# Two transformer blocks on one core: index scores issued in pairs of heads, four more weight loads whose low halves come by transfer, and block 2's memory attention with its outputs laid out by features

## The reference, cut to what matters

```python
    for layer in range(DEPTH):
        h = rmsnorm_2(x, norm_mix[layer])
        hq, hf, hi, hg, sq, sk, sv, iq, ik, iw, mq = split_in(h @ w_in[layer])
        o_hg = hgrn2_mix(hq, hf, hi, hg, lb[layer], hg_out_gain[layer])
        o_sa = dsa_mix(sq, sk, sv, iq, ik, iw, sa_q_gain[layer], sa_k_gain[layer])
        o_mem = mem_mix(mq, rmsnorm_2(mem, norm_mem[layer]), w_mem_kv[layer],
                        mem_q_gain[layer], mem_k_gain[layer])
        x = x + jnp.concatenate([o_hg, o_sa, o_mem], -1) @ w_out[layer]

# dsa_mix, for each block of 128 queries
        s = jnp.einsum('bqhd,bsd->bqhs', iqb, ik32)
        score = jnp.einsum('bqh,bqhs->bqs', iwb, jax.nn.relu(s))
# mem_mix
    logits = jnp.einsum('bqhd,bmhd->bhqm', qm, km) * (MEM_DH_2 ** -0.5)
    p = jax.nn.softmax(logits, axis=-1)
    out = jnp.einsum('bhqm,bmhd->bqhd', p, vm)
```

## Time and profile before

| | |
|---|---|
| median of 3 runs | 1542.08 us (1541.72 to 1542.87) |
| the profiled execution, its time | 1541.8 us |
| the profiled execution, its span | 1540.0 us |
| TensorE busy | 1521.7 us, 99% |
| VectorE busy | 860.6 us, 56% |
| ScalarE busy | 641.3 us, 42% |
| GpSimd busy | 24.1 us, 2% |
| DMA, mean | 103 GB/s |

### The profile page before, as it was taken

One profiled execution on the slowest core, in us unless ns is written; L12 is line 12 of the kernel. 1 busy time (PEld: TensorE's weight loads), 2 busy tenths in 40 slices (PEclk: granted clock), 3 DMA queues, 4 the chain that ended last, 5 costly groups with the idle time before them and its releaser, 6 DMA issues. The chain is left out here.

```text
span 1540.0 us, 20083 instructions
## 1 busy us (share of the span) xinstructions
PE 1521.7 (99%) x7670; PEld 1268.5 (82%) x7670; DVE 860.6 (56%) x1321; ACT 641.3 (42%) x888; POOL 24.1 (2%) x32
## 2 busy tenths in 40 slices
PE   7999999999999999999999999999999999999999
PEld 7888667888888888888888868999888888888887
DVE  5443565444456877777434778878564543444222
ACT  6442444322245444444333555686653322322210
POOL 0000000000000000000000000010000000000000
PEclk9999999999999999999999999999999999999999
DMA  9313212232233133222333223254312322222232
GB/s 363 132 55 109 103 56 82 83 109 94 98 113 133 55 110 109 83 107 82 137 109 128 69 83 113 56 124 106 91 65 82 110 84 107 87 103 96 95 109 82
DMA packets 25386, 158.33 MB, mean 103 GB/s; under 512 B 2819, under 2 KB 3331, under 8 KB 8300
## 3 DMA queue, kind: packets, MB, share of 16 engines
q1 hardware_dynamic: 23228, 150.01, 27.5%
q0 software_dynamic: 2016, 7.34, 2.5%
q10 hardware_dynamic: 80, 0.13, 0.0%
HBM read 147.87 MB, written 2.13 MB: 97 GB/s over the span
## 5 line engine op out<-in xcount | busy, mean ns | idle before, releaser
L1202 DVE TENSOR_TENSOR w_lo<-raw,w_hi 128x2048 fp32r<-128x2048 f32 x109 | 249.8, 2292 | 347.3 <-ACT w_hi L644 347.2
L1952 PE MATMUL bank<-h_hi,w_hi 128*128 128x512 f32 x1096 | 431.5, 394 | 1.1 <-DVE cy L1544 0.8
L1954 PE MATMUL bank<-h_hi,w_lo 128*128 128x512 f32 x1096 | 427.0, 390 | 0.0
L1953 PE MATMUL bank<-h_lo,w_hi 128*128 128x512 f32 x1096 | 426.7, 389 | 0.0
L644 ACT ACTIVATE w_hi<-raw 128x2048 fp32r<-128x2048 f32 x123 | 235.0, 1910 | 321.7 <-PE bank L1954 307.4
L1952 PEld LDWEIGHTS bank<-h_hi,w_hi 128*128 128x128 f32 x1096 | 205.6, 188 | 45.3 <-issue 2.8
L1954 PEld LDWEIGHTS bank<-h_hi,w_lo 128*128 128x128 f32 x1096 | 205.3, 187 | 43.7
L1953 PEld LDWEIGHTS bank<-h_lo,w_hi 128*128 128x128 f32 x1096 | 205.5, 188 | 42.0 <-issue 0.2
L1952 PE MATMUL bank<-a_hi,w_hi 128*128 128x512 f32 x352 | 136.9, 389 | 0.0
L1953 PE MATMUL bank<-a_lo,w_hi 128*128 128x512 f32 x352 | 136.9, 389 | 0.0
L1954 PE MATMUL bank<-a_hi,w_lo 128*128 128x512 f32 x352 | 136.9, 389 | 0.0
(11 more groups left out here) (315 smaller groups left out, 2005.2 us busy)
## 6 DMA issues: line engine op xcount, KB each, us to landing
raw<-weights SPq DMA_DIRECT2D x128, 1024.0 KB, 4.8
w_lo<-raw POOLq DMA_DIRECT2D x14, 512.0 KB, 5.0
toep<-bias_scratch SPq DMA_DIRECT2D x8, 448.0 KB, 4.6
x<-xT SPq DMA_DIRECT2D x2, 1024.0 KB, 12.7
x_tok<-x_tok SPq DMA_DIRECT2D x1, 2048.0 KB, 13.8
mem2T<-mem2T SPq DMA_DIRECT2D x2, 1024.0 KB, 5.3
outT<-x SPq DMA_DIRECT2D x8, 256.0 KB, 4.2
lead<-lead SPq DMA_DIRECT2D x2, 512.0 KB, 4.7
```

Source lines behind the costliest of these rows:

```text
L1202: nc.vector.tensor_tensor(w_lo[PLACE[m]][:, :], raw[m % 2][:, :], w_hi[PLACE[m]][:, :].bitcast(F32), ALU.subtract).then_inc(lo_ready, 1)
L1952: nc.tensor.matmul(o, lh, rh, start=first, stop=False)
L1953: nc.tensor.matmul(o, lh, rl, start=False, stop=False)
L1954: return nc.tensor.matmul(o, ll, rh, start=False, stop=last)
```

## The change

- `BY_DMA` begins at `hq` instead of `mq`. So both loads of `hq`, `sq` and `sk` get their low halves by ScalarE's negative copy and GpSimd's transfers, and VectorE's four `split_w` go. GpSimd's two memsets of `ik` go as well. Its other memsets now stand between the first transfers.
- Index scores: `ik` has the keys in both halves of its rows, with no zeros. Two heads are issued together, each on its own 64 rows. After each pair TensorE does two of the 24 products that remain of `hf`. VectorE's split of `hf`'s second load, the scaling of `hf` and three rounds of `top_keys` move in between the pairs; ScalarE rounds and negates the first `hq` load near pair 6.
- Memory attention: the transposed probabilities of two heads are collected over four query blocks (`pT_pair`). At steps 11 and 19 four matmuls make the outputs of two heads, 64 features by 512 tokens each. The inverse sums are spread by four transposes at steps 10 and 18. The 16 `O` of `mem_2` and the two `mix_turn` at steps 32 and 33 go.

```diff
-BY_DMA = range(FIRST["mq"], FIRST["w_out_2"] + 1)
+BY_DMA = range(FIRST["hq"], FIRST["w_out_2"] + 1)
...
@@ gpsimd
+            add_lows(0, 1)
             pool.wait_ge(*completion(("turn_km", 1)))
             nc.gpsimd.memset(kmT[1][0:64, :, :], 0.0).then_inc(padded, 1)
             pool.wait_ge(padded, 3)
+            add_lows(1, 2)
             pool.wait_ge(log_used, 1)
             nc.gpsimd.memset(skT[1][0:64, :, :], 0.0).then_inc(padded, 1)
             pool.wait_ge(padded, 4)
...
+            add_lows(2, len(BY_DMA))
@@ scalar
+                if w == 13:
+                    round_w(FIRST["hq"])
+                if w in (14, 15):
+                    minus_part(FIRST["hq"], w - 14)
...
             for m in range(2):
-                round_w(FIRST["hf"] + m + 2)
+                if m:
+                    round_w(FIRST["hq"] + 1)
+                    for part in range(2):
+                        minus_part(FIRST["hq"] + 1, part)
                 for t in (2 * m, 2 * m + 1):
                     wait_own(("hf", t))
                     nc.scalar.activation(abs_z[:, t * S:(t + 1) * S], lf[:, t * S:(t + 1) * S], ACT.Abs
...
             for m in range(2):
                 round_w(FIRST["hq"] + m + 2)
+                for part in range(2):
+                    minus_part(FIRST["hq"] + m + 2, part)
@@ vector
+            def between_scores(pair_):
+
+                if pair_ in (1, 2):
+                    split_part(FIRST["hf"] + 1, pair_ - 1)
+                if pair_ in (3, 5, 9):
+                    t = {3: 0, 5: 1, 9: 2}[pair_]
+                    ready(("hf", t))
+                    normal("hf", t, lf[:, t * S:(t + 1) * S])
+                if pair_ == 4:
+                    dve.wait_ge(relu_used, IDXH + 2)
+                    hide_later(1)
+                if pair_ in (6, 10, 11):
+                    r = {6: 0, 10: 1, 11: 2}[pair_]
+                    top_keys(r, r + 1)
...
+                    if s in (2 * TT + 1, 4 * TT + 1):
+                        f = (s - 1) // (2 * TT) - 1
+                        dve.wait_ge(exp_ready, UNIT0["mem_2"] + 2 * TT * (f + 1))
+                        link(nc.vector.reciprocal(sums[:, f, :], sums[:, f, :]))
+                        nc.vector.tensor_copy(inverse_2[:, :].rearrange("p (u d) -> p u d", d=64),
+                                              sums[:, f, :].unsqueeze(2).to_broadcast([P, 2 * TT, 64])
+                                              ).then_inc(inverse_2_ready, 1)
@@ tensor
+                    if s in (2 * TT + 2, 4 * TT + 2):
+                        f = (s - 2) // (2 * TT) - 1
+                        claim(("R2", f))
+                        pe.wait_ge(inverse_2_ready, f + 1)
+                        for i in range(TT):
+                            ins = nc.tensor.transpose(B(("R2", f))[:, i * P:(i + 1) * P],
+                                                      inverse_2[:, i * P:(i + 1) * P], ident[:, :])
+                        done(("R2", f), ins)
+                    if s in (2 * TT + LAG, 4 * TT + LAG):
...
+                        for c in range(MT):
+                            for e in range(2):
+                                h = 2 * f + e
+                                ins = nc.tensor.matmul(B(("O2", f))[64 * e:64 * e + 64, :],
+                                                       vm[:, c, h * DH:(h + 1) * DH], pT_pair[e][:, c, :],
+                                                       start=c == 0, stop=c == MT - 1)
...
-            for w_, (i, h) in enumerate(IDX):
-                claim(("idx", w_))
-
-                done(("idx", w_), nc.tensor.matmul(B(("idx", w_))[:, 0:P * (i + 1)], iq[:, h // 2, i * P:(i + 1) * P],
-                                                   ik[h % 2][:, 0:P * (i + 1)], start=True, stop=True))
+            for w_ in range(0, len(IDX), 2):
+                for e in range(2):
+                    claim(("idx", w_ + e))
+                for e in range(2):
+                    i, h = IDX[w_ + e]
+                    rows_ = slice(64 * e, 64 * e + 64)
+                    done(("idx", w_ + e), nc.tensor.matmul(
+                        B(("idx", w_ + e))[:, 0:P * (i + 1)], iq[rows_, h // 2, i * P:(i + 1) * P],
+                        ik[rows_, 0:P * (i + 1)], start=True, stop=True))
+                for p_ in (KT + w_, KT + w_ + 1):
```

More of the change, by code:

```diff
@@ L254, in plan_banks @@
     tiles("o_hg", TT, (TAIL_BANK,))
-    tiles("turn_mix", KT)
+    for j in range(2, KT):
+        use(("turn_mix", j), j % 4)
     tiles("w_out_2", KT, (4, 5, 0, 1), first=FIRST["w_out_2"], per=2)
@@ L373, in build @@
         v_hg = at("v_hg", AR + 32 * K, [TT, S])
-        ik = [at(f"ik{s}", AR + (40 + 2 * s) * K, [S]) for s in range(2)]
+        ik = at("ik", AR + 40 * K, [S])
         relu = [at(f"relu{s}", AR + (44 + 2 * s) * K, [S]) for s in range(2)]
@@ L397, in build @@
         row_2 = [at(f"row_2{s}", AR + (72 + 2 * s) * K, [S]) for s in range(NLP)]
+        pT_pair = [at(f"pT_pair{e}", AR + (20 + 24 * e) * K, [MT, S]) for e in range(2)]
+        inverse_2 = at("inverse_2", AR + 96 * K, [S])
         pT_2 = [at(f"pT_2{s}", AR + (46 + 50 * s) * K, [TT, P]) for s in range(2)]
@@ L456, in build @@
         padded = sem("padded")
[L457 removed]
+        iw_rows, ik_odd_in = sem("iw_rows"), sem("ik_odd_in")
         half_rms = sem("half_rms")
@@ L580, in _, with add_lows @@
         def _(pool):
+            def add_lows(first, last):
+                for n_ in range(first, last):
+                    m = BY_DMA[n_]
+                    if n_:
+                        pool.wait_ge(lo_added, 32 * n_)
+                    for part in range(2):
+                        cut = slice(part * SLOT // 2, (part + 1) * SLOT // 2)
+                        pool.wait_ge(minus_hi, 2 * n_ + part + 1)
+                        nc.gpsimd.dma_start(w_lo[PLACE[m]][:, cut], raw[m % 2][:, cut], accum_op=ALU.add
+                                            ).then_inc(lo_added, 16)
             nc.gpsimd.memset(ones[:, :], 1.0).then_inc(set_up, 1)
@@ L1702, in _ @@
             wait_free(("iw", 0))
[L1703 to L1715, removed]
             def top_keys(first, last):
@@ L1727, in top_keys, with hide_later @@
                         link(nc.vector.tensor_scalar(scores, scores, TAKEN, NEG, ALU.not_equal, ALU.mult))
-            for m in range(2):
-                if m == 0:
-                    split_w(FIRST["hf"] + 1)
-                for t in (2 * m, 2 * m + 1):
+            def hide_later(i):
+                cut = sel[:, i, P * i:P * (i + 1)]
+                link(nc.vector.tensor_tensor(cut, cut, causal[:, :], ALU.add))
+            def between_scores(pair_):
[3 more added lines that the diff above has]
+                    t = {3: 0, 5: 1, 9: 2}[pair_]
                     ready(("hf", t))
                     normal("hf", t, lf[:, t * S:(t + 1) * S])
-                split_w(FIRST["hf"] + m + 2)
-                top_keys(5 * m, 5 * m + 5)
+                if pair_ == 4:
[4 more added lines that the diff above has]
+                    top_keys(r, r + 1)
+            for w, (i, h) in enumerate(IDX):
+                keys = P * (i + 1)
+                wait_free(("idx", w))
+                if w:
+                    dve.wait_ge(relu_used, w)
+                nc.vector.scalar_tensor_tensor(out=sel[:, i, 0:keys], in0=relu[w % 2][:, 0:keys],
+                                               scalar=iw[:, i, h:h + 1], in1=sel[:, i, 0:keys], op0=ALU.mult,
+                                               op1=ALU.add).then_inc(relu_used, 1)
+                if w % 2:
+                    between_scores(w // 2)
+            dve.wait_ge(relu_used, len(IDX))
+            for i in (2, 3):
+                hide_later(i)
+            ready(("hf", 3))
+            normal("hf", 3, lf[:, 3 * S:4 * S])
+            top_keys(3, 10)
             for m in range(2):
@@ L2422, in _ @@
             pe.wait_ge(ik_odd_in, 16)
[L2423 to L2434 removed]
+            for w_ in range(0, len(IDX), 2):
[8 more added lines that the diff above has]
+                for p_ in (KT + w_, KT + w_ + 1):
+                    t, kt = divmod(p_, KT)
+                    ld, key, cs = FIRST["hf"] + t // 2, ("hf", t), slice(t % 2 * P, (t % 2 + 1) * P)
+                    if kt == 0:
+                        weights(ld)
+                        claim(key)
+                    ins = product(B(key)[:, :], w(ld, 1)[:, kt, cs], w(ld, 0)[:, kt, cs], h_hi[:, kt, :], h_lo[:, kt, :],
+                                  kt == 0, kt == KT - 1)
+                    if kt == KT - 1:
+                        done(key, ins)
+            turn_heads("turn_km", km_tok, M)
             feature_loads("hq", 2)
```

85 lines of the change are left out of this document (57 added, 28 removed).

## The result

The changed kernel took 1548.16 us (median of 6 runs, 1547.21 to 1550.42), the kernel before 1541.9 us beside it (6 runs, 1541.1 to 1542.87). The ratio is 1.0043, with a 95% interval from 1.0033 to 1.0053. The forecast was 1541.7 with a range from 1536 to 1545.

A forecast was written before the change was run, and what follows sets the result against it. The prediction took the kernel to be bound by TensorE's order of work almost everywhere (busy 99%). From 1541.8, +2.0 up to the first level and -2.4 in attention gave 1541.4, plus 0.3 for the median 1541.7; range 1536 to 1545.

The forecast's parts named there:

- Index scores, -3.1 us: Index scores: issuing heads in pairs takes 12.6 us instead of 15.7, so `hq` starts 3.1 us earlier.
- VectorE and ScalarE keep up: Index scores: both engines keep pace, as a pair with six products takes TensorE 2.2 us or more.
- on no path: VectorE's four dropped splits, 4 x 2.3 = 9.2 us, were said to hold up nothing.
- The second `hq` load, 2.5 us: Low half lands at 941.3 but TensorE wants it at 938.8, so it waits 2.5 us.
- The lower estimate: Skill-based time of 4.4 us for two transfers; both waits would nearly vanish. The forecast kept to the rows instead.
- `sq`, 3.0 us, at 955.3: GpSimd issues `sq`'s transfer behind a memset at 948.0; it lands at 955.3 and TensorE waits another 3.0 us.
- The 0.3 us for `tok`: TensorE's 0.3 us wait for `tok` behind `sq` was expected to vanish.
- the forecast of +2.0: Net up to the first level: 2.0 us slower, from the index gain, the two transfer waits and `tok`.
- The rival that had 0.10: Clock falls in the waits, 2.5 us per slow stretch: 1546.7, or 1547.2 with slower transfers and one fall; chance 0.10.
- Attention, -2.4 us: Memory attention: sixteen `O` save 7.3 us, added transposes cost 0.9 and new outputs 4.0; net 2.4 us less.
- The rival "the attention gain does not come": ScalarE's extra copies and VectorE's `top_keys` pace shorter steps in memory attention: 1544.1; chance 0.11.
- `mix_turn`, 0: Two `mix_turn` of 0.44 us each go; nothing booked, since TensorE's next transposes wait for VectorE's scaling.

The follow-up runs named there:

- e9: e5 with three rounds of `top_keys` moved from in front of the first level to behind its `self` products; 1538.61 us, ratio 0.9978.
- e3: Kernel before with index pairs alone: all four low halves by VectorE as before, old memory attention; 1542.78 us, ratio 1.0003.
- e5: e3 with the fourth tile of `sq` in bank 3 instead of bank 0; 1546.17 us, ratio 1.0018.
- e7: e6 with ScalarE rounding and negating the second `hq` load ahead of the memory key copies and first two absolute values; 1543.76 us, ratio 1.0006.
- e1: Kernel before with the new memory attention alone; 1544.62 us, ratio 1.0019.
- e8: e1 with ScalarE's copy of `R2` and VectorE's product over `O2` at their steps' start, two `top_keys` rounds later; 1541.53 us, ratio 0.9996.
- e2: Changed kernel with the old memory attention; index pairs and the four added low halves by transfers stay; 1545.73 us, ratio 1.0024.
- e4: Kernel before with only the four low halves moved from VectorE to transfers; 1546.77 us, ratio 1.0032.
- e6: e2 with `sq`'s transfers issued ahead of the memset and the fourth tile of `sq` in bank 3; 1543.24 us, ratio 1.0005.
- e12: e11 with `sq`'s low half by transfers too, issued ahead of the memset; both `hq` loads keep VectorE's subtraction; 1539.06 us, ratio 0.9984.
- e11: e9 with e8's memory attention, and `sk` alone of the four loads getting its low half by transfers; 1537.66 us, ratio 0.9973.

## Why the prediction was wrong

- **Index scores, -3.1 us.** Right as a size: the pairs start 2.2, 2.4 and 2.6 us apart, `hq` starts at 927.79 where 927.8 was forecast, and e9 gets the gain in full. Wrong as a gain that is simply there. "VectorE and ScalarE keep up" was worked out for the pairs alone. Up to the first level the two have a chain of their own (logarithm, `qf`, `kk`, `z`, masked copies), and it had little slack left: e3 and e5 show the same wait at two places, for ScalarE and for VectorE. Nor were the splits plainly "on no path". In e5, which keeps them, VectorE is full up to the first level and TensorE waits 2.28 us for it; in the changed kernel, without them, VectorE stood idle for 2.29 us there, waiting for ScalarE's `z`.
- **The second `hq` load, 2.5 us.** Measured 2.45, at 941.40 where 941.3 was forecast, for the reason given; e7 takes ScalarE's order away and the wait goes. The lower estimate that the prediction set beside it, 4.4 us for the two transfers, is not what was measured (7.2), and it would not have made both waits nearly vanish: issued at 948.1, `sq` would have landed at 952.5, and without the first wait TensorE wants it at 938.8 + 11.0 = 949.8.
- **`sq`, 3.0 us, at 955.3.** It starts at 955.31, but the wait is 1.08: the clock's fall had used up 1.8 of the rest. The landing was right, and so was the memset's part: the transfers were issued at 948.11, and 7.2 us later `sq` went on.
- **The 0.3 us for `tok` "should vanish".** It is 1.04. ScalarE's copy of `tok` began at 964.72, 3.2 us later than before (961.52), while `sq` was 2.4 late: the rounding of `sk` began 1.1 us later, and behind it `sk`'s two negative copies (2.0 us) now stand in front of `qf`, `kk` and `z`. Before, then in the changed kernel:

```profile
953.21 1.91 ACT L644 ACTIVATE w_hi<-raw 128x2048 fp32r<-128x2048 f32 x1 [5.72 <-PE bank L1954]
...
961.52 1.21 ACT L682 ACTIVATE tok<-bank,st 128x256 f32<-128x256 f32 x3
...
954.32 1.91 ACT L654 ACTIVATE w_hi<-raw 128x2048 fp32r<-128x2048 f32 x1 [5.66 <-PE bank L2026]
956.27 2.01 ACT L661 ACTIVATE w_lo<-w_hi 128x1024 fp32r<-128x1024 f32 x2
...
964.72 1.20 ACT L692 ACTIVATE tok<-bank,st 128x256 f32<-128x256 f32 x3
```

This step failed, and it is most of the 1.5 us by which the first stretch (3.5) misses the forecast of +2.0: the new copies were priced on the way to the transfers, and not for what is queued behind them.
- **The clock.** The rival that had 0.10 was right that the clock falls, and wrong in its price: one fall and 1.8 us in the trace, not 2.5. Its 2.5 came from slow matmuls at the start of the kernel; the profile's rows have a granted clock of 1.00 for that stretch, so they don't show it at 1.2 GHz. Its time for one fall (1547.2) is near the 1548.16 measured, but by luck: 3.0 us of it are slower transfers, which took 7.2 us as forecast, and the loss in the attention isn't in it. Its "no row shows a fall behind so short a wait" was a lack of rows, not evidence. In this kernel it came out within the wait for `sq`, so it moved the end little; in e3 and e5 it decided the result.
- **Attention, -2.4 us.** Measured +2.8. This is the step that failed most, 5.2 of the 6.5 us between forecast and result: "VectorE's new reciprocals, copies and products [...] stay beside TensorE's work". The costs on TensorE were right: `R2` takes 0.6, `O2` 1.94 against 2.0, and e1's waits (1.8, 1.4, 1.2, 0.7) add up to 5.1, so the work itself is 2.3 us shorter. What was not looked at is that both new outputs pass through one bank (`O_BANK`), in turn with ScalarE's copy and VectorE's product, and that VectorE is full of `top_keys` there. The rival "the attention gain does not come" had the right cause and stopped at a gain of nothing, for no reason: a wait can cost more than the edit saves. The order can be mended (e8), but only 0.7 us of the gain comes then.
- **`mix_turn`, 0.** Right: the transposes start at 1135.82, behind VectorE's scaling (from 1133.59, 2.18 long).

What stays open: why the clock fell behind a wait of 2.3 us in seven executions of eleven in e3 and not in the other four, and why it stayed down for 3.4 us in six traces (the changed kernel, e2, e3, e4, e6, e7) and for 10.2 in e5. The waits of 0.7 us at the end of the attention weren't tried. With VectorE's order mended the transfers were tried for `sk` and `sq` alone, and not for the two loads of `hq`.

## What to carry to other kernels

Where one engine is busy 99% of the time, ask of each microsecond that is taken from it how much slack the other engines' longest chain has at the next place where they meet: here it was about one microsecond, and 3 us of saving needed two small moves elsewhere to come through. A new result that TensorE must wait for is priced by the queue that makes it and by the bank that it passes through, not by its own duration. A long chain (10.8 us from rounding to landing) is free only for a load that is wanted well over that time after its place comes free; for `sk`, with 18.6 us, it was free, and for `sq`, with 11, a start 1.1 us late was enough for a wait.

## What the runs showed of the hardware

- TensorE's granted clock fell to 0.50 behind waits of 2.3 to 2.7 us in seven profiled executions (the changed kernel and e2 to e7), and not behind those of 1.0 (e12) and 1.8 us (e1) in the executions profiled. In the changed kernel TensorE had been at work again for 1.4 us when it fell. It cost 1.8 us there and in e3, and 3.3 to 5.5 in e5.
- Shorter waits are not cleared by that. Two unprofiled executions of e1, one of e8, one of e11 and three of e12 have a mean clock of 0.999 and are 1.0 to 2.1 us above their medians; no trace shows where it was lower. The kernel before has 1.000 in every execution run beside the experiments.
- The same wait did not always bring it: 7 executions of 11 in e3, 9 of 11 in e5. So the medians of such kernels mix two times, and have to be read beside each execution's clock.
- A pair of 512 KB adding transfers took 7.2 to 7.3 us from GpSimd's first issue to TensorE's next product, and the whole chain from rounding 10.8, 10.8 and 10.9 us in three places (`hq` in the changed kernel, `sq` in e7 and in e12).
